# One step of a head norm moved, and one map of exponentials left in PSUM, in a two-layer hybrid decoder

## The reference

```python
p = jax.nn.softmax(s, axis=-1)
a = (p[:, :, 0] - lam * p[:, :, 1]).astype(v.dtype)
o = einsum('bhqk,bkhe->bqhe', a, v)
o = o * rsqrt(mean(square(o), axis=-1) + LN_EPS)   # per head
o = o * norm_g * (1.0 - lam_init)
```

## Time and profile before

| | |
|---|---|
| median of the runs | 2024.99 us |
| the profiled execution's own time | 2022.58 us |
| its span, first to last instruction | 2020.8 us |
| mean granted TensorE clock | 0.987 of full speed |
| DVE busy | 1103.0 us |
| ACT busy | 708.5 us |
| POOL busy | 324.3 us |

### The profile page before, as it was taken

How to read it: one execution, slowest core, us unless ns; L and a number is a source line. 1 busy time by engine, 2 the same in 40 slices (tenths; PEclk the granted TensorE clock), 3 DMA queues, 4 the chain that set the end, 5 groups by cost and what they waited for, 6 DMA issues and landing times.

```text
span 2020.8 us, 25257 instructions
## 1 busy us (share of the span) xinstructions
PE 1943.2 (96%) x9341; PEld 1625.9 (80%) x9341; DVE 1103.0 (55%) x1792; ACT 708.5 (35%) x1023; POOL 324.3 (16%) x287
## 2 busy tenths in 40 slices
PE   7999999999899999999999999999999899999996
PEld 6888888888777888888888888888877788888885
DVE  6544444654876544444574444446567775444446
ACT  4233232344544333323232222224454352332321
POOL 6100000153313400000150000003432251000002
PEclk9999999999989999999999999999998999999998
DMA  5222222236722222222322222232576122222221
GB/s 222 104 83 104 83 104 104 92 120 186 189 71 82 107 104 83 104 83 104 115 104 83 104 83 104 83 145 66 152 200 162 37 105 103 83 104 83 104 104 42
DMA packets 41922, 216.99 MB, mean 107 GB/s; under 512 B 8724, under 2 KB 9172, under 8 KB 17928
## 3 DMA queue, kind: packets, MB, share of 16 engines
q1 hardware_dynamic: 38984, 200.35, 28.2%
q0 software_dynamic: 2880, 15.90, 3.4%
HBM read 198.28 MB, written 17.93 MB: 107 GB/s over the span
## 4 chain that ended last, share of the span: by engine, by line
PE 86%; DVE 7%; issue 2%; ACT 2%; DMA 1%; SPq 1%; POOL 0%; DVEq 0%; ACTq 0%; POOLq 0%
PE bank L887 78%; PE bank L1050 3%; PE bank L1146 1%; DVE res L1317 1%; DMA rawA<-in_a_w 1%; PE bank L915 1%; DVE st L1341 1%; PE bank L1134 1%; DVE hl L1577 1%; ACT s L811 1%; DVE negm L1550 1%; PE bank L1148 1%; DVE nat L1542 1%; PE bank L1122 1%; DVE hl L1392 0%
## 5 line engine op out<-in xcount | busy, mean ns | idle before, releaser
L887 PE MATMUL bank<-whiD,hl 128*128 128x512 f32 x1408 | 444.0, 390 | 3.9 <-DVE hl L1392 3.5
L1317 DVE SCALAR_TENSOR_TENSOR res<-bank,res 128x512 f32<-128x512 f32 x384 | 258.5, 688 | 175.4 <-PE bank L887 173.4
L887 PEld LDWEIGHTS bank<-whiD,hl 128*128 128x128 f32 x1408 | 264.3, 188 | 62.4 <-DVE hl L1392 5.6
L887 PE MATMUL bank<-xhi,whiA 128*128 128x512 f32 (+1 forms) x768 | 288.0, 375 | 10.3 <-DVE xlo L1296 10.3
L887 PE MATMUL bank<-xlo,whiA 128*128 128x512 f32 (+1 forms) x768 | 286.3, 373 | 0.0
L887 PE MATMUL bank<-xhi,wloA 128*128 128x512 f32 (+1 forms) x768 | 286.2, 373 | 0.0
L887 PE MATMUL bank<-wloD,hl 128*128 128x512 f32 x704 | 274.0, 389 | 0.0
L887 PE MATMUL bank<-xhi,whiB 128*128 128x512 f32 x704 | 273.9, 389 | 0.0
L887 PE MATMUL bank<-xlo,whiB 128*128 128x512 f32 x704 | 273.9, 389 | 0.0
L887 PE MATMUL bank<-xhi,wloB 128*128 128x512 f32 x704 | 273.9, 389 | 0.0
L887 PEld LDWEIGHTS bank<-xhi,whiA 128*128 128x128 f32 x768 | 145.8, 190 | 38.0 <-DVE xlo L1296 8.5
(11 more groups left out here) (183 smaller groups left out, 3128.3 us busy)
## 6 DMA issues: line engine op xcount, KB each, us to landing
rawA<-in_a_w SPq DMA_DIRECT2D x63, 1024.0 KB, 4.7
rawB<-in_b_w SPq DMA_DIRECT2D x54, 1024.0 KB, 4.7
rawD<-in_d_w SPq DMA_DIRECT2D x46, 1024.0 KB, 4.8
stacks<-hl SPq DMA_DIRECT2D x192, 64.0 KB, 1.7
whiD<-stacks POOLq DMA_DIRECT2D x10, 768.0 KB, 6.3
wloD<-stacks POOLq DMA_DIRECT2D x10, 768.0 KB, 5.9
gbr<-in_gb_row SPq DMA_DIRECT2D x7, 1024.0 KB, 7.5
stacks<-wloD SPq DMA_DIRECT2D x48, 64.0 KB, 1.7
```

Of the source, the lines that this page charges most:

```text
L887: ins = t_.matmul(out_, a_, b_, start=(start and k == 1), stop=(stop and k == n), skip_group_check=check)
L1317: v.scalar_tensor_tensor(out=r, in0=bank[b][:, :], scalar=scale, in1=r, op0=ALU.mult, op1=ALU.add).then_inc(step, 1)
```

## The change

There are two edits.

The first gives `RMS_AT` a list for each body. Only one number differs: in body 4 stage 3 of `rms` runs at the end of step 5, no longer at the end of step 6.

The second is about the second map of a differential step. Its exponentials are written over the scores in PSUM (`bank[i]`), no longer to `s32`. `mix` reads them there. The weight `wlam` is made by a `tensor_scalar` with two scalars taken from SBUF, in place of a `scalar_tensor_tensor` whose second tensor was `nlam1`. PE may write the bank anew when `mix` has read it, so its two waits on `exp_ok[1]` become waits on `mixp_ok`.

```diff
-RMS_AT = (2, 3, 4, 6)
+RMS_AT = {2: (2, 3, 4, 6), 4: (2, 3, 4, 5)}
...
-                        a.activation(s32[:, i, 0:w], bank[i][:, 0:w], ACT.Exp, bias=negm[:, i:i + 1],
+                        a.activation(bank[i][:, 0:w] if m else s32[:, i, 0:w], bank[i][:, 0:w], ACT.Exp, bias=negm[:, i:i + 1],
                                      accum_out=rsum[:, i:i + 1]).then_inc(exp_ok[m], 1)
...
-                        pe.wait_ge(exp_ok[1], (l + 1) * DIFF_P * STEPS)
+                        pe.wait_ge(mixp_ok, (l + 1) * DIFF_P * STEPS)
...
-                            pe.wait_ge(exp_ok[m], count(l, G - 2, m))
+                            pe.wait_ge(mixp_ok if m else exp_ok[0], count(l, G - 2, m))
...
-                    v.scalar_tensor_tensor(out=wlam[:, j:j + 1], in0=rinv[:, j, 1:2], scalar=rsum[:, i:i + 1],
-                                           in1=nlam1[:, :], op0=ALU.mult, op1=ALU.mult).then_inc(wlam_ok, 1)
+                    v.tensor_scalar(wlam[:, j:j + 1], rinv[:, j, 1:2], rsum[:, i:i + 1], nlam1[:, :],
+                                    ALU.mult, ALU.mult).then_inc(wlam_ok, 1)
...
-                    v.scalar_tensor_tensor(out=s32[:, i, 0:w_], in0=s32[:, i + 1, 0:w_], scalar=wlam[:, j:j + 1],
+                    v.scalar_tensor_tensor(out=s32[:, i, 0:w_], in0=bank[i + 1][:, 0:w_], scalar=wlam[:, j:j + 1],
                                            in1=s32[:, i, 0:w_], op0=ALU.mult, op1=ALU.add).then_inc(mixp_ok, 1)
...
-                    if b - 1 in DIFF_AT and k in RMS_AT:
-                        rms(DIFF_AT.index(b - 1), RMS_AT.index(k))
+                    if b in RMS_AT and k in RMS_AT[b]:
+                        rms(DIFF_AT.index(b - 1), RMS_AT[b].index(k))
```

## The result

The changed kernel takes 2008.57 us (median of 4 runs, 2007.66 to 2009.37) against 2024.53 us for the kernel before (4 runs). The ratio is 0.9929, with a 95% interval of 0.9916 to 0.9941. On the forecast's own scale 2024.99 us x 0.9929 is 2010.6 us, which is the forecast. That it fits to the tenth is luck: the plain quotient of the two medians above is 0.9921, or 16.0 us gained, and the profiled execution has a span of 2007.3 us, 13.5 less than before, where 14.4 was forecast.

The account below looks back on a forecast made before the run. PE, busy 96% of the span, was taken as the bound. The move's 7.6 + 6.1 - 0.4 = 13.3 us plus 1.1 for the second map gave 14.4: 2024.99 - 14.4 = 2010.6 us, range 2008 to 2017.

Parts of the forecast that it names:

- The cause of the wait: At each attention's end, L1542's four gain products crawl beside POOL's SBUF reads: 5.22 us against 0.89 elsewhere.
- The waits that go, 7.6 us, and the clock, 6.1 us: At both attention ends, PE idle of 3.03, 3.04, 0.59 and 0.97 us goes; half-speed losses of 3.2 and 2.9 go too.
- The cost of the move, 0.4 us: In step 6 DVE's work comes 0.8 us later, so `values(37)` starts 0.2 us late in each of two layers.
- The stretch behind the last scores: From the last scores to the first late product at the attention's end: 7.9 us in place of 14.
- Edit 2, 1.1 us: Over 32 differential steps, the second map in PSUM gains 1.9 us on the weight and loses 0.8 on its scalar.
- rival B: The new one-element weight L1567 is still held by POOL, so 1.9 us do not come: 2012.5 us; chance 32%.
- The release: Weight L1567 in differential steps no longer held by POOL: gain 0 to 2.1 us, 1.9 taken.
- the second scalar: The weight's extra scalar from SBUF costs 63 ns each, in some 13 waits: 0.8 us lost, bounds 0 and 2.0.
- The exponentials: ACT writing second maps to PSUM: taken as 0, bounds 8.9 us lost to 1.3 us gained.
- C: The clock falls all the same near the attention ends, from remaining waits; 6.1 us do not come: 2016.7 us; chance 9%.
- E: Exponentials over their own scores run at half rate; from about 2 us of idle the clock falls: 2031 us; chance 3%.
- D: Something behind the attention, such as a weight split or load, runs by its own time; PE meets it sooner: 2017; 9%.

Follow-up runs that it names:

- the first and the third experiment: Two changes to the kernel before: gain products alone moved to step 5, 2009.36 us (0.9935); or POOL's late weights made to wait for them at step 6, 2007.92 us (0.9931).
- the third experiment: Kernel before, norm still at step 6, with one wait added on POOL: late weights' low half starts only after the gain products; 2007.92 us, ratio 0.9931.
- the key experiment: Changed kernel with the last pair's key split put ahead of that step's exponentials on ACT and mix on DVE, in body 3; 2005.68 us, ratio 0.9916.
- the version with both orders: Changed kernel with the early key split, and with the low part ahead of the mix in 384 and 512 wide differential steps; 2002.44 us, ratio 0.9902.

## Why the prediction was right

- **The cause of the wait.** L1542 beside POOL: right. Moving either of the two (the first and the third experiment) gives 13 and 14 us. This agrees with the rule of the Trainium skill, SBUF — State Buffer, section "Who interferes with whom", that an instruction with two inputs in SBUF contends with POOL's reads: 5.22 us beside POOL, 0.89 without.
- **The waits that go, 7.6 us, and the clock, 6.1 us.** Right as a sum: less the 0.4 us of the move they are 13.3, and it was 13.6 us by the timelines, 13.1 by the runs. The clock's part was measured by itself as 6 us.
- **The cost of the move, 0.4 us.** PE starts `values(37)` at 1591.98, 0.47 after the product before it (1591.51). From one such product to the next it is 0.23, so PE waits some 0.24 in this layer. Right.
- **The stretch behind the last scores** was said to become 7.9 us and is 6.9. The terms of the sum gave 7.2, from 13.9 less 6.7; the 7.9 was carried over wrongly. The sum did not use it.
- **Edit 2, 1.1 us.** The traces give 1.0, the runs 0.0 within 1.8 us, so it is shown by single traces alone. Its terms were right in kind and a little off in size. The weight is not held: right, against rival B. The two-port rule of the Trainium skill on the same page hangs on conditions on the operands; this one-element instruction does not show it. The release gave 1.3 us (body 1 with the weight in its old form against the new), where 1.9 less the second scalar's share was taken. The second scalar costs 53 ns (272 for 219) where 63 was taken, and the loss of 0.4 us in the two bodies 3 is most likely its work. The exponentials were taken as nothing, and nothing is what they give to whoever waits for them. The Trainium skill, ScalarE: Activation LUTs, says that ACT is faster into PSUM; the trace agrees for the instruction itself (652 ns for 681), but the small gain in time that would follow from it did not come.
- **Rivals.** C fell: the clock is 1.00 in both ends. Its premise was too simple all the same, and so was E's point at about 2 us of idle: in the key experiment waits of 2.00 and 1.87 us left the clock at 1.00. D fell in the stretch itself: no wait in the late output. E fell: no row at half rate. What remains is that the ends and edit 2 make 14.6 us and the spans of the two profiled executions differ by 13.5. PE's waits for L1392 in the feed-forward parts, which neither edit touches, are 3.5 us before and 5.1 after; over the kernels here they lie between 3.5 and 5.2, also with the first edit out. I take that for scatter between executions, and have not tested it.

## What to carry to other kernels

When an instruction takes almost six times its usual length, look at which other engine starts at that moment before looking at its own queue: here either of the two could step aside. Where the rows show the clock fall behind a PE wait, price the wait with the slow clock behind it, which here cost about as much again at the ends of the attention (3 us of wait, 3 us of clock). Where another engine is close behind PE, a part of the clock's return turns into a longer wait. And when an instruction gets shorter, look at when the next one that waits for it starts: here the exponentials were 29 ns shorter and nothing came sooner. An edit that frees one instruction from a shared resource hands the hold to the next one of its kind, so the chain has to be freed as a whole.

## What the runs showed of the hardware

- In the attention the clock fell to 1.2 GHz at PE waits of 1.8 to 3.0 us and never at those of up to 1.2 us. But not at each of the longer ones: in the second layer of the key experiment and of the version with both orders it stayed at 1.00 through waits of 2.0 and 1.9 us, while in the first layer of both it fell behind one of 2.0. The length of the wait is not the whole rule; what else goes in was not tested.
- The window view prints a granted clock of 1.00 from 20 to 24 us of the changed kernel, behind waits of 3.92 and 2.22 us, and it is not to be believed there. Products of one kind start 0.21 us apart up to 24 us and 0.12 apart behind it, which is the slow clock and then the full one. Where a clock matters, look at the distances of the products too.

```profile
23.35 0.41 PE L887 MATMUL bank<-xlo,whiA 128*128 128x256 f32 x1
23.56 0.41 PE L887 MATMUL bank<-xhi,wloA 128*128 128x256 f32 x1
...
24.51 0.28 PE L887 MATMUL bank<-xhi,wloA 128*128 128x256 f32 x1
24.63 0.28 PE L887 MATMUL bank<-xhi,whiA 128*128 128x256 f32 x1
```

- ACT writes exponentials over their own input in one PSUM bank at the rate at which it writes them to SBUF: 332 ns at 128 wide, 652 at 512, so 0.83 ns an element.
- A `tensor_scalar` of one element with two scalars from SBUF takes 272 ns beside a POOL instruction that reads SBUF, the same as without one; a `scalar_tensor_tensor` with a second input in SBUF in its place took up to 845 (in the third experiment), usually 220.
